# Unread identity products ahead of TensorE's waits, and a rebuilt first norm, in a two-model transformer kernel

## The reference, cut to what matters

```python
silu_c, silu_cc = silu(c), silu(c_ctx)
m  = silu_c  @ ada_w[0] + ada_b[0]        # shift and scale of the latent tokens
mc = silu_cc @ ada_w[0] + ada_b[0]        # the same for the context tokens
h  = rms_norm(x,   norm_mix[0]) * (1.0 + sc_m)  + sh_m
hc = rms_norm(ctx, norm_mix[0]) * (1.0 + csc_m) + csh_m
o, oc = even_mixer(h, hc, even_w_in[0], ...)   # projections of h and hc, the gates' 16 columns among them
```

## Time and profile before

| | |
|---|---|
| runs | 3719.12, 3721.03, 3727.19 us, median 3721.03 us |
| profiled execution | 3728.01 us, span 3726.2 us |
| mean granted TensorE clock | 0.97 of 2.4 GHz |
| TensorE busy | 3491.7 us, 94% |
| VectorE, ScalarE, GpSimd busy | 40%, 34%, 31% |
| first product of item 2 of the front | 74.13 us after the start |

### The profile page before, as it was taken

How to read it: one execution, slowest core, us unless ns; L and a number is a source line. 1 busy time by engine, 2 the same in 40 slices (tenths; PEclk the granted TensorE clock), 3 DMA queues, 4 the chain that set the end, 5 groups by cost and what they waited for, 6 DMA issues and landing times.

```text
span 3726.2 us, 60251 instructions
## 1 busy us (share of the span) xinstructions
PE 3491.7 (94%) x24164; PEld 3027.9 (81%) x24164; DVE 1503.2 (40%) x2665; ACT 1261.2 (34%) x1831; POOL 1170.4 (31%) x812
## 2 busy tenths in 40 slices
PE   6998878889999999999999999998999999989998
PEld 4777768777888888888778888978999988777887
DVE  5966644433221122555532124454312244552121
ACT  2544422222111112355534223254422232544222
POOL 1221112213222233111145453223444432234453
PEclk8999989989999999899999999999999999999999
DMA  4310000002432311111123221111222211112222
GB/s 194 130 68 29 31 1 2 2 13 79 167 127 78 146 65 59 35 46 40 47 79 102 89 103 67 63 46 63 74 100 81 101 63 57 46 68 90 96 96 90
DMA packets 65309, 273.56 MB, mean 73 GB/s; under 512 B 9840, under 2 KB 10992, under 8 KB 62064
## 3 DMA queue, kind: packets, MB, share of 16 engines
q1 hardware_dynamic: 61120, 268.04, 20.2%
q10 hardware_dynamic: 4016, 3.03, 0.3%
HBM read 268.95 MB, written 2.10 MB: 73 GB/s over the span
## 4 chain that ended last, share of the span: by engine, by line
issue 52%; PE 21%; POOL 19%; DVE 6%; ACT 1%; POOLq 0%; DMA 0%; ACTq 0%; SPq 0%; DVEq 0%
POOL w_lo L366 18%; PE ps L378 9%; PE ps L1078 4%; DVE arena L1370 1%; DVE arena L1356 1%; PE ps L1170 1%; PE ps L1588 1%; PE ps L1594 0%; PE ps L1148 0%; PE ps L1161 0%; PE ps L1497 0%; PE ps L1158 0%; DMA resid<-in_xT 0%; POOLq L361 0%; POOL delta_bufs L1877 0%
## 5 line engine op out<-in xcount | busy, mean ns | idle before, releaser
L366 POOL TENSOR_TENSOR w_lo<-raw,w_hi 128x512 fp32r<-128x512 f32 (+1 forms) x760 | 1097.9, 1466 | 2281.2 <-ACT w_hi L315 2281.2
L315 ACT CAST w_hi<-raw 128x1024 fp32r<-128x1024 f32 (+1 forms) x380 | 419.7, 1105 | 1476.7 <-PE ps L378 1174.4
L378 PE MATMUL ps<-act_hi,w_hi 128*128 128x512 f32 (+2 forms) x2304 | 653.5, 338 | 19.1 <-POOL w_lo L366 13.5
L378 PE MATMUL ps<-act_lo,w_hi 128*128 128x512 f32 (+2 forms) x2304 | 650.8, 337 | 0.0
L378 PE MATMUL ps<-act_hi,w_lo 128*128 128x512 f32 (+2 forms) x2304 | 650.7, 337 | 0.0
L378 PEld LDWEIGHTS ps<-act_hi,w_hi 128*128 128x128 f32 x2304 | 405.3, 188 | 83.1 <-issue 22.7
L378 PEld LDWEIGHTS ps<-act_hi,w_lo 128*128 128x128 f32 x2304 | 407.5, 188 | 48.0
L378 PEld LDWEIGHTS ps<-act_lo,w_hi 128*128 128x128 f32 x2304 | 407.3, 188 | 45.2
L514 DVE TENSOR_TENSOR nscr<-nscr,ps 128x512 f32<-128x512 f32 (+2 forms) x132 | 69.6, 555 | 847.9 <-PE ps L378 824.9
L378 PE MATMUL ps<-ff_lo,w_hi 128*128 128x512 f32 (+2 forms) x1056 | 297.0, 335 | 0.0
L378 PE MATMUL ps<-ff_hi,w_lo 128*128 128x512 f32 (+2 forms) x1056 | 297.0, 335 | 0.0
(11 more groups left out here) (436 smaller groups left out, 5575.0 us busy)
## 6 DMA issues: line engine op xcount, KB each, us to landing
raw<-in_gu SPq DMA_DIRECT2D x176, 512.0 KB, 3.2
arena<-in_ada SPq DMA_DIRECT2D x24, 2048.0 KB, 8.3
raw<-in_dn SPq DMA_DIRECT2D x64, 704.0 KB, 4.0
raw<-in_in SPq DMA_DIRECT2D x56, 512.0 KB, 3.2
raw<-in_even_in SPq DMA_DIRECT2D x28, 512.0 KB, 3.3
raw<-in_odd_in SPq DMA_DIRECT2D x24, 512.0 KB, 3.2
raw<-in_out SPq DMA_DIRECT2D x16, 512.0 KB, 3.2
raw<-in_even_out SPq DMA_DIRECT2D x8, 512.0 KB, 3.3
```

Source lines behind the costliest of these rows:

```text
L315: act.copy(w_hi[:, j, 0:cols], raw[:, j, 0:cols]).then_inc(s["hi_ready"], 1)
L366: ins = pool.tensor_tensor(w_lo[:, j, c], raw[:, j, c], w_hi[:, j, c].bitcast(F32), ALU.subtract)
L378: mm = pe.matmul(ps[:, 2 * j + b, 0:cn], wt[:, j, w], acts[:, k, c0:c0 + cn], start=(k == 0 and wt is w_hi and acts is hi), stop=(k == kt ...
```

## The change

1. **Products of the identity with itself.** A helper `hold(pe, beats, bank)` issues `beats` float32 products of the 128 x 128 identity with itself into a piece of PSUM that nobody reads. It is called ahead of TensorE's waits (in `post` and behind the fresh products of `pe_gate_up` too), with a number of beats written out for each place. Outside the opening 392 beats are issued in one execution: 106 in the seven norms (2, 3 and 13 in the two norms over all tokens, 2, 3 and 9 in the other five), 68 ahead of the turns at items 36, 42, 48, 52 and 54 of the front (where PE now also waits for `front_read` first), 16 ahead of three of its items, 48 in seven of its events, 16 at its end, 17 behind the gates' tables, 18 in the first step of the delta rule, 21 in `post`, 12 in `near`, 26 in the two `second` stages, 20 ahead of three out-projections and 24 behind the first products of three gate-and-up stages.
2. **The opening.** Setup waits for the vectors and constants alone. The order of the modulation weights on the host changes, so that each DMA group holds two shift blocks and the two scale blocks of the same two tiles. PE issues 36 identity products first, then sums each tile's squares with products 2 columns wide straight from the squares (48 of them in place of 12; DVE's additions go), and everything behind runs by tiles: spread rows, DVE's product, ACT's scale and shift (in place of DVE's), ACT's rounding, DVE's subtraction. The gates' products run tile by tile between them. `stage("small_split")` comes ahead of `open`. The first weight block's DMA is issued behind the first group's.

```diff
+            sp.dma_start(vec[:, :], dram["vecs"]).then_inc(s["setup_landed"], 16)
+            sp.dma_start(base[:, :], dram["base"]).then_inc(s["setup_landed"], 16)
             sp.dma_start(x[:, :, 0:CTX], dram["ctxT"]).then_inc(s["inputs_landed"], 16)
             sp.dma_start(x[:, :, CTX:T], dram["xT"]).then_inc(s["inputs_landed"], 16)
             for i in range(4):
                 sp.dma_start(ada_ring[:, i, :], dram["ada"][i]).then_inc(ada_landed[i], 16)
-            for j in range(SLOTS):
-                sp.dma_start(raw[:, j, 0:FULL], dram["even_in"][j]).then_inc(w_landed[j], 16)
+                if i in (0, 3):
+                    j = i // 3
+                    sp.dma_start(raw[:, j, 0:FULL], dram["even_in"][j]).then_inc(w_landed[j], 16)
 ...
+        def hold(pe, beats, bank):
+
+            for _ in range(beats):
+                pe.matmul(ps[:, bank, 3 * P:4 * P], ident, ident, start=True, stop=True)
+
 ...
+                begun = n.pop("begun")
+                hold(pe, 4 if begun else 8, 7)
                 pe.wait_ge(s["lo_ready"], b0 + 1)
                 pe.wait_ge(s["tile_read"], read0 + SLOTS)
-                pe_products_fresh(pe, halves, fresh, n.pop("begun"), b0 + SLOTS)
+                pe_products_fresh(pe, halves, fresh, begun, b0 + SLOTS)
 ...
                     pe_products_fresh(pe, halves, fresh)
+                    if halves[-1][0] + halves[-1][1] - halves[0][0] < T:
+                        hold(pe, 8, 7)
 ...
                 pe.matmul(ps[:, 7, 2 * i:2 * i + 2], nscr[:, 3, c:c + P], ones[:, 0:2], start=True, stop=True)
+            hold(pe, 2, 4)
             pe.wait_ge(s["squares_ready"], n.at("squares_ready") + KD)
 ...
             mm.then_inc(s["norm_sums"], 1)
+            hold(pe, 3, 4)
             pe.wait_ge(s["norm_scale"], n.at("norm_scale") + 1)
             for i, (c, cn) in enumerate(chunks):
                 mm = pe.matmul(norm_row[:, P * i:P * i + cn], norm_scales[:, 2 * i:2 * i + 1].to_broadcast([P, P]), ident[:, P - cn:P],
                                start=True, stop=True)
             mm.then_inc(s["norm_rows"], 1)
+            hold(pe, 13 if len(chunks) > 5 else 9, 7)
 ...
+        def open_squares(k):
+            return nscr[:, k % 4, 0:T]
+
+        def open_tile(k):
+            return nscr[:, (4, 5, 0, 1)[k % 4], 0:T]
+
+        open_sums = ps[:, 7, 0:16 * KD]
+        gate_sums = [ps[0:16, b, 0:3 * P] for b in (3, 7)]
 ...
+            def sums(k):
+                pe.wait_ge(s["squares_ready"], k + 1)
+                for i, (c, _) in enumerate(chunks):
+                    mm = pe.matmul(ps[:, 7, 16 * k + 2 * i:16 * k + 2 * i + 2], open_squares(k)[:, c:c + P], ones[:, 0:2], start=True, stop=True)
+                mm.then_inc(s["squares_added"], 1)
+
+            def group(r):
+                if r:
+                    pe.wait_ge(s["ada_rows"], r)
                 pe.wait_ge(ada_landed[r], 16)
-                pe_ada_products(pe, ada_ring[:, r, :], 2 + r % 2)
+                pe_ada_products(pe, ada_ring[:, r, :], 2)
             def turn(r):
                 pe.wait_ge(s["ada_rows"], r + 1)
+                if r:
+                    pe.wait_ge(s["ada_read"], r)
                 pe_ada_turn(pe, ada_front[:, r, :], 6, 8 * r)
+
+            def tile(k):
+                w = slice(k * P, (k + 1) * P)
+                pe.wait_ge(s["parts_ready"], k + 1)
+                for h, (c0, cn) in enumerate(BOTH):
+                    for wt, a in ((w_hi, act_hi), (w_hi, act_lo), (w_lo, act_hi)):
+                        mm = pe.matmul(ps[:, h, 0:cn], wt[:, 0, w], a[:, k, c0:c0 + cn],
+                                       start=(k == 0 and wt is w_hi and a is act_hi), stop=(k == KD - 1 and wt is w_lo))
+                    if k == KD - 1:
+                        mm.then_inc(s["front_done"], 1)
+
+            def gate_products(k):
+                for q in range(2):
+                    for w, a in ((ws_hi, act_hi), (ws_hi, act_lo), (ws_lo, act_hi)):
+                        mm = pe.matmul(gate_sums[q], w[:, k, 0:16], a[:, k, 3 * P * q:3 * P * (q + 1)],
+                                       start=(k == 0 and w is ws_hi and a is act_hi), stop=(k == KD - 1 and w is ws_lo))
+                if k == KD - 1:
+                    mm.then_inc(s["gates_rows"], 1)
 ...
+            for _ in range(36):
+                pe.matmul(ps[:, 0, 3 * P:4 * P], ident, ident, start=True, stop=True)
+            for k in range(5):
+                sums(k)
+            group(0)
+            for k in range(5, KD):
+                sums(k)
+            turn(0)
 ...
             mm.then_inc(s["norm_rows"], 1)
-            turn(0)
-            products(2)
+            group(1)
+            pe.wait_ge(s["lo_ready"], 1)
+            tile(0)
             turn(1)
-            products(3)
+            tile(1)
+            pe.wait_ge(s["small_parts"], 1)
+            gate_products(0)
+            group(2)
+            tile(2)
+            gate_products(1)
             turn(2)
+            tile(3)
+            gate_products(2)
+            group(3)
+            gate_products(3)
             turn(3)
+            tile(4)
+            for k in range(5, KD):
+                tile(k)
+                gate_products(k - 1)
+            gate_products(KD - 1)
         def act_open(act, n):
+            act.activation(small[:, 94:95], eps_ap, ACT.Sqrt)
+            act.wait_ge(s["inputs_landed"], 32)
             for k in range(KD):
-                if k >= 2:
-                    act.wait_ge(s["squares_added"], k - 1)
-                act.activation(nscr[:, k % 2, 0:T], x[:, k, :], ACT.Square).then_inc(s["squares_ready"], 1)
+                if k >= 4:
+                    act.wait_ge(s["squares_added"], k - 3)
+                act.activation(open_squares(k), x[:, k, :], ACT.Square).then_inc(s["squares_ready"], 1)
+
+            def tile(k):
+                act.wait_ge(s["rows_scaled"], k + 1)
+                act.wait_ge(s["open_mod"], k // 2 + 1)
+                if k >= 4:
+                    act.wait_ge(s["parts_ready"], k - 3)
+                for h0, hn in BOTH:
+                    z = 1 if h0 == 0 else 0
+                    ins = act.activation(open_tile(k)[:, h0:h0 + hn], open_rows(k)[:, h0:h0 + hn], ACT.Identity,
+                                         bias=mod[:, k, z:z + 1], scale=amod[:, 0, k, z:z + 1])
+                ins.then_inc(s["scaled_ready"], 1)
+                act.wait_ge(s["scaled_ready"], k + 1)
+                act.copy(act_hi[:, k, :], open_tile(k)).then_inc(s["modulated"], 1)
 ...
+            group_rows(0)
 ...
+            act_split(act, 0, 16, FULL)
+            tile(0)
+            group_rows(1)
+            tile(1)
+            tile(2)
+            group_rows(2)
+            tile(3)
+            tile(4)
+            group_rows(3)
+            tile(5)
+            act_split(act, 1, 16, FULL)
+            tile(6)
+            tile(7)
 ...
+            w = 2 * len(norm_chunks(BOTH))
+
+            def rows(k):
+                dve.tensor_tensor(open_rows(k), x[:, k, :], norm_row[:, 0:T], ALU.mult).then_inc(s["rows_scaled"], 1)
+
+            def modulation(r):
+
+                dve.wait_ge(s["ada_turned"], r + 1)
+                b = v("ada_b", 0, 16).rearrange("p (a g q) -> p g a q", a=2, g=4)[:, r]
+                m = mod[:, 0:16, :].rearrange("p (a g q) z -> p g a q z", a=2, g=4)[:, r]
+                dve.tensor_tensor(m, ps[:, 6, 8 * r:8 * r + 8].rearrange("p (a q z) -> p a q z", a=2, q=2),
+                                  b.unsqueeze(3).to_broadcast([P, 2, 2, 2]), ALU.add).then_inc(s["ada_read"], 1)
+                dve.wait_ge(s["ada_read"], r + 1)
+                dve.scalar_tensor_tensor(amod[:, 0, 2 * r:2 * r + 2, :], mod[:, 8 + 2 * r:10 + 2 * r, :], 1.0,
+                                         v("norm_mix", 2 * r, 2).unsqueeze(2).to_broadcast([P, 2, 2]), ALU.add, ALU.mult).then_inc(s["open_mod"], 1)
+
+            def low(k):
+                dve.wait_ge(s["modulated"], k + 1)
+                dve.tensor_tensor(act_lo[:, k, :], open_tile(k), act_hi[:, k, :].bitcast(F32), ALU.subtract).then_inc(s["parts_ready"], 1)
+
+            dve.wait_ge(s["inputs_landed"], 32)
+            dve.wait_ge(s["squares_added"], KD)
+            dve.tensor_reduce(norm_totals[:, 0:w], open_sums.rearrange("p (a c) -> p c a", a=KD)[:, 0:w], AX.X, ALU.add).then_inc(s["norm_total"], 1)
+            modulation(0)
+            dve.wait_ge(s["norm_root"], 1)
+            dve.reciprocal(norm_scales[:, 0:w], norm_roots[:, 0:w]).then_inc(s["norm_scale"], 1)
+            dve.wait_ge(s["norm_rows"], 1)
+            rows(0)
+            rows(1)
+            rows(2)
+            low(0)
+            modulation(1)
+            low(1)
+            rows(3)
+            rows(4)
+            low(2)
+            modulation(2)
+            low(3)
+            rows(5)
+            rows(6)
+            rows(7)
+            low(4)
+            modulation(3)
+            low(5)
+            low(6)
```

(44 more changed lines are left out.)

104 lines of the change are left out of this document (21 added, 83 removed).

## The result

The changed kernel takes 3716.48 us (median of 20 runs, 3709.97 to 3721.49) against 3723.11 us for the kernel before (median of 20 runs, 3718.29 to 3729.57) on the same chip: ratio 0.9981, 95% interval 0.9975 to 0.9987. That is 6.6 us, where 47.6 us were forecast, and it lies outside the range. The profiled execution took 3711.7 us.

What follows compares the result with a forecast made beforehand. It took TensorE, busy 94% of the span and partly at half clock, to bound the kernel. Clock 42.6 us plus opening 7 us less beats 2 us gave 3721.0 - 47.6 = 3673.4 us, range 3646 to 3708 us.

Steps and rivals of the forecast that it cites:

- The clock is held by unread identity products.: Behind the opening: mean clock 0.985 or more, under 100 us at half clock in place of 195 us.
- 3.4 us or none: Sign behind each norm: a half-clock stretch this long in place of 10.2 us.
- The slower rival: Beats don't hold the clock up and cost 0.43 us each at half clock, overhanging their waits: 3742 us, chance 0.09.
- the falls only move: Rival: the clock still falls in norms and around narrow products, one third of 56.8 us gained: 3699 us, chance 0.23.
- Three quarters of 56.8 us, 42.6 us: Gain from running TensorE's 21 half-clock stretches near beats at full clock, 56.8 us at most; ends 15 and 65 us.
- I add 2 us: Cost of the 392 beats outside the opening, 0.22 us each, almost all inside existing waits; ends 0 and 10 us.
- Cost nothing: The added waits for `front_read` at five turns and `post_y` three times were to cost no time.
- a gain of 7 us: Opening: item 2 starts at 67 us in place of 74.1 us; ends 10 us gained, 1 us lost.
- three times for the norm rows: Opening: norm rows ready at about 34.5, 39.5 or 45 us with full, midway falling or half clock.
- Roots and spread rows, some 3 us: Opening: time for these behind the sums and one group's products, before norm rows are ready.
- 30 us behind the norm rows: Opening: when the new chain by tiles ends, drawn out, against 35.1 us in the old chain.
- It starts from the first items and moves forward as a whole, so the gain stays.: VectorE's convolution work behind the opening: it was to keep the opening's gain of 7 us.

Runs made afterwards that it cites:

- experiment 1: The changed kernel with the opening of the kernel before and all 392 beats kept: 3710.09 us, ratio 0.9960.
- experiment 7: The kernel before with only the 209 beats from the closing projection on, the norms' among them: 3718.33 us, ratio 0.9985.
- experiments 8 and 9: Old opening, 348 beats: 8 doubled the beats behind the norms, 3706.62 us; 9 instead replaced VectorE's subtraction in the norms with a one-input operation, 3693.43 us.
- experiment 6: The kernel before with only the 139 beats from the front's item 36 to the delta rule: 3713.53 us, ratio 0.9976.
- experiment 2: The changed kernel with its rebuilt opening and added waits, but no beats behind the opening: 3731.36 us, ratio 1.0018.
- experiment 11: The changed kernel without the 44 early beats, its opening reordered (TensorE's groups 2 and 3 and ScalarE's row copies earlier): 3701.36 us, ratio 0.9942.
- experiment 12: The kernel of experiment 11 with 18 of the 36 products ahead of the opening's sums: 3703.32 us, ratio 0.9942.

## Why the prediction was wrong, step by step

- **The clock is held by unread identity products.** Right: 0.989 (0.985 or more was named), 55 us at half clock (under 100), against 195 us. One sign was missed: in place of 3.4 us or none, two of the norms still have some 7 us at half clock (884.8 and 1496 us). And "ten of the forty slices" below full speed was misread: the line shows four; nothing in the sum hangs on it. The slower rival is out, and so is "the falls only move". The Trainium skill, page "TensorE: Matmul & The Clock Gate", Part 1, on ramping up costing under 1% of a span, comes out nearer than the forecast: the beats gave back 0.40% with the old opening. No run shows whether its reason is the one found here.
- **"Three quarters of 56.8 us, 42.6 us".** As TensorE's own busy time it was nearly right: 49.3 us in experiment 1, or 40.6 us with overlaps counted once. As time of the kernel it failed: all beats together gave 14.1 us. The step that failed is the one that turned busy time at half clock into time of the span: its bound of 56.8 us carried the caution "a busy TensorE that somebody else holds up would gain nothing", and only a quarter was taken off for it and for the narrow products together. Behind the norms and in the stages around them most of it was held up: 24.0 us saved, 19.9 us returned (experiment 7), where VectorE's pace of 1.42 us a tile is what holds TensorE (experiments 8 and 9). The forecast never set the six products of a tile at half clock beside VectorE's two operations for a tile; a view of both engines behind one norm of the kernel before would have given 1.4 us for each.
- **"I add 2 us" for the beats.** The price was near: 101.6 / 392 = 0.26 us in place of 0.22. Some ran at half clock, and the row counts overlaps too: nine beats at full clock stand in it with 2.26 us, 0.25 us each, and with overlaps counted once all of them are 92.9 / 392 = 0.24 us. Site by site they fit the waits of before at full clock, but not where they start at half: in the first norm 13 beats took 3.92 us against a wait of 3.66 us, which is what the slower rival described, in small. But TensorE's waits are not fixed: with its work at full clock it comes sooner to the next one, so 101.6 us of beats took the place of only 68.3 us of idleness. That is the same 33.3 us, seen from the other side. Of it some 20 us lie from the closing projection on (experiment 7), 7.7 us at the beats of experiment 6 (33.4 us, idle time 25.7 us less), and the early beats have most of the rest. These are single executions: that of experiment 6 was 18.5 us shorter than that of the kernel before, where the medians give 10.4 us, so its 7.7 us are the least certain. Which engine holds TensorE up at the turns was not tested as it was behind the norms.
- **The added waits.** "Cost nothing" was said of the waits for `front_read` and `post_y`. No run has them alone; experiment 2 leaves them some 2 us at most. The turns' waits fell to 1.1 us at most, near the 1 us named; before the first products of the delta rule 2.1 us stay, not under 1 us.
- **The opening, "a gain of 7 us".** Wrong in sign: 5.2 us lost. The beats end at 19.66 us, as forecast, and the sums take 12.4 us, inside the two ends. Its three times for the norm rows don't add up: 20 us and the terms named give 35.1, 40.9 and 46.6 us, where 34.5, 39.5 and 45 us stand. Measured were 41.76 us. Two steps failed. "Roots and spread rows, some 3 us" were 6.1 us (35.63 to 41.76): a turn at half clock and the modulation's two small operations stand ahead of VectorE's reciprocal, and the spread rows ran at half clock. And "30 us behind the norm rows" held for the work, not for the order that was written: ScalarE stands 5.71 us behind group 2 with tile 3 queued behind it, which needs group 1 alone, and 4.52 us behind group 3 with tile 5, which needs group 2. In the order of experiment 11 it is 29.6 us.
- **"It starts from the first items and moves forward as a whole, so the gain stays."** Not so: VectorE's convolution pace depends on when GpSimd's splits fall. The changed kernel lost 2.7 us more there by 208 us, and experiment 12 loses there all that it wins in the opening.
- **The sum.** Forecast -42.6 - 7 + 2 = -47.6 us. Measured, by the ratios: 0.40% or 14.9 us faster for beats and clock (experiment 1), less 0.21% or 7.8 us for the opening, leaves 7.1 us; the medians of the changed kernel give 6.6 us. So the two terms for beats and clock, -40.6 us together, were off by some 26 us, and the opening's by some 15 us.

## What to carry to other kernels

Time at half clock is worth what TensorE's products gain on the engine that feeds them, not half of the busy time: set the group of products and the feeder's operations for it side by side, and count only where TensorE is the longer. When a filler goes into a wait, the ledger (own work, filler, idle time) of the whole span tells whether it replaced idleness or made it; the medians must say how much time that is. In a written-out order, look for an engine that waits for something the tiles behind it don't need; one reordering here was worth 9 us, where the 44 early beats and the 36 opening products cost time or gave none.

## What the runs showed of the hardware

A VectorE step with two SBUF inputs, 128x770, takes 1.02 us alone and some 1.93 us when it begins while GpSimd subtracts a weight block; one that already runs when the subtraction begins keeps its 1.02 us (at 181.8 us in the kernel before, with 0.9 us beside the split). The Trainium skill, page "GPSIMD Engine Reference", section 1, says that GpSimd's SBUF interfaces are shared with VectorE, with contention for instructions with two SBUF inputs; the trace agrees and gives the size, 0.9 us a step. Blocks of the same work were 11.15 us and 13 us long, and the short ones stood right behind a fall of TensorE's clock: so, as far as these coincidences show, a slower clock made the kernel locally faster.

A slack engine absorbs a surprising amount: 71 more products, an estimated 15.6 us by their price of 0.22 us, changed the time by 0.6 us. And the clock can fall right behind beats: in the changed kernel's first norm TensorE ran 12 records 2 columns wide in 1.40 us, 2 beats, idled for 0.38 us and began 12 more such records, and from 884.8 to 892.5 us, without a gap, the clock is at 0.56.
